# Turning four operands of a chunked recurrence by transpositions where identity products stood

## What is computed

```python
def step(S, inp):
    r_t, w_t, k_t, v_t, a_t, b_t = inp
    sa = jnp.einsum('bhij,bhj->bhi', S, a_t)
    S = S * w_t[:, :, None, :] + sa[..., None] * b_t[:, :, None, :] + v_t[..., None] * k_t[:, :, None, :]
    y = jnp.einsum('bhij,bhj->bhi', S, r_t)
    return S, y
y = _rwkv7_scan(rh, decay, kh, vh, -kk, kk * ah)
```

## Time and profile before

| | us |
|---|---|
| median of three runs | 3031.03 |
| the profiled execution | 3030.16 |
| its span, first to last instruction | 3028.1 |
| PE busy (matmul) | 2707.8 (89%) |
| PE weight loads busy | 2233.2 (74%) |
| DVE / ACT / POOL busy | 1236.1 / 771.9 / 287.3 |
| recurrence, first to last PE instruction | some 265, from 2563 to 2828 |
| TensorE's mean granted clock | 0.944 |

### The profile page before, as it was taken

One profiled execution on the slowest core, in us unless ns is written; L12 is line 12 of the kernel. 1 busy time (PEld: TensorE's weight loads), 2 busy tenths in 40 slices (PEclk: granted clock), 3 DMA queues, 4 the chain that ended last, 5 costly groups with the idle time before them and its releaser, 6 DMA issues. The chain is left out here.

```text
span 3028.1 us, 49010 instructions
## 1 busy us (share of the span) xinstructions
PE 2707.8 (89%) x20661; PEld 2233.2 (74%) x20661; DVE 1236.1 (41%) x2017; ACT 771.9 (25%) x1452; POOL 287.3 (9%) x193
## 2 busy tenths in 40 slices
PE   9799999999987898869999999997998987777766
PEld 8799999999965655758888888875776862676455
DVE  6333333333342567262333333336233334454437
ACT  6221111111151178242111111112211122323221
POOL 1100000000030034020000000005000000222102
PEclk9899999999988999989999999998999996899878
DMA  4211111111036400331111111103202100000032
GB/s 141 77 42 62 43 42 42 42 61 44 22 121 148 166 2 2 114 122 56 42 42 42 62 42 51 54 28 132 71 21 84 49 19 8 4 4 4 4 118 97
DMA packets 59995, 175.92 MB, mean 58 GB/s; under 512 B 10046, under 2 KB 17631, under 8 KB 58672
## 3 DMA queue, kind: packets, MB, share of 16 engines
q1 hardware_dynamic: 59826, 173.47, 17.5%
HBM read 146.50 MB, written 26.36 MB: 57 GB/s over the span
## 5 line engine op out<-in xcount | busy, mean ns | idle before, releaser
L771 PE MATMUL f0gu<-b1XH,f0w0H 128*128 128x346 f32 (+1 forms) x528 | 170.4, 323 | 12.6 <-DVE f0w0L L699 12.6
L773 PE MATMUL f0gu<-b1XH,f0w0L 128*128 128x346 f32 (+1 forms) x528 | 170.6, 323 | 0.0
L725 DVE TENSOR_TENSOR Y<-f0dn,Y 128x512 f32<-128x512 f32 (+1 forms) x180 | 123.9, 689 | 113.7 <-PE f0dn L795 112.7
L772 PE MATMUL f0gu<-b1XL,f0w0H 128*128 128x346 f32 (+1 forms) x528 | 169.9, 322 | 0.0
L773 PE MATMUL f0gu<-b1XH,f0w1L 128*128 128x346 f32 (+1 forms) x528 | 169.7, 321 | 0.0
L771 PE MATMUL f0gu<-b1XH,f0w1H 128*128 128x346 f32 (+1 forms) x528 | 169.3, 321 | 0.0
L714 DVE TENSOR_TENSOR f1hf<-f1sg,f1gu 128x512 f32<-128x512 f32 x44 | 30.2, 687 | 340.4 <-ACT f1sg L667 340.4
L772 PE MATMUL f0gu<-b1XL,f0w1H 128*128 128x346 f32 (+1 forms) x528 | 169.0, 320 | 0.0
L714 DVE TENSOR_TENSOR f0hf<-f0sg,f0gu 128x346 f32<-128x346 f32 (+1 forms) x66 | 34.1, 516 | 329.4 <-ACT f0sg L667 329.4
L771 PE MATMUL f1gu<-b1XH,f1w0H 128*128 128x512 f32 x352 | 139.0, 395 | 12.0 <-DVE f1w0L L699 12.0
L725 DVE TENSOR_TENSOR Y<-f1dn,Y 128x512 f32<-128x512 f32 x160 | 109.2, 690 | 90.6 <-PE f1dn L795 90.6
(11 more groups left out here) (387 smaller groups left out, 6512.2 us busy)
## 6 DMA issues: line engine op xcount, KB each, us to landing
f0raw<-in_w_gate_up SPq DMA_DIRECT2D x44, 512.0 KB, 5.6
f1raw<-in_w_gate_up SPq DMA_DIRECT2D x44, 512.0 KB, 5.2
residual<-Y SPq DMA_DIRECT2D x32, 512.0 KB, 2.8
Y<-in_w_ada SPq DMA_DIRECT2D x8, 1536.0 KB, 6.6
f0rawd<-in_w_down SPq DMA_DIRECT2D x22, 512.0 KB, 3.4
f1rawd<-in_w_down SPq DMA_DIRECT2D x22, 512.0 KB, 3.4
w_in_b_raw<-in_w_in_b SPq DMA_DIRECT2D x17, 512.0 KB, 3.4
w_in_a_raw<-in_w_in SPq DMA_DIRECT2D x12, 512.0 KB, 4.4
```

Source lines behind the costliest of these rows:

```text
L725: dve.tensor_tensor(y, dn[0:r, (par * ND + i) % 4], y, ALU.add).then_inc(s["acc"], 1)
L771: pe.matmul(o, wH[c][:, j, k], xh, start=(k == 0), stop=False)
L772: pe.matmul(o, wH[c][:, j, k], xl, start=False, stop=False)
L773: last = pe.matmul(o, wL[c][:, j, k], xh, start=False, stop=(k == KC - 1))
```

## The change

In `inverse_start` the blocks of chunk 0, whose outputs lie on partitions 0 to 63, become transpositions; those of chunk 1 stay products with the identity. In `turn`, an even head's two chunks become one transposition of a 64x128 block, whose output covers all 128 partitions. An odd head's chunk 1, whose output lies on partitions 0 to 63, becomes a 64x64 transposition; its chunk 0 stays a product. The order within a (pair, operand) is: transposition, transposition, product. Waits and marks stay as they are.

```diff
                         for q in range(2):
                             for e in range(2):
                                 o = H * c
-                                mm = pe.matmul(wk[rows(q), e, o:o + H], XT(t, e, c, q), cst[at(e, q), 1, 0], start=True, stop=True)
+                                if q:
+                                    mm = pe.matmul(wk[rows(q), e, o:o + H], XT(t, e, c, q), cst[at(e, q), 1, 0], start=True, stop=True)
+                                else:
+                                    mm = pe.transpose(wk[rows(q), e, o:o + H], XT(t, e, c, q), cst[at(e, q), 1, 0])
                     pa.mark(mm, "tx")
...
                     for c in range(4):
                         for i, src in enumerate(pair):
-                            for q in range(2):
-                                for e in range(2):
-                                    mm = pe.matmul(wk[at(e, q), e, 4 * H * i + H * c:4 * H * i + H * (c + 1)], src[rows(e), c, chunk(t, q)], b.ident[rows(e), rows(e)], start=True, stop=True)
+                            o = slice(4 * H * i + H * c, 4 * H * i + H * (c + 1))
+                            pe.transpose(wk[:, 0, o], src[rows(0), c, tok(t)], b.ident[rows(0), rows(0)])
+                            pe.transpose(wk[at(1, 1), 1, o], src[rows(1), c, chunk(t, 1)], b.ident[rows(1), rows(1)])
+                            mm = pe.matmul(wk[at(1, 0), 1, o], src[rows(1), c, chunk(t, 0)], b.ident[rows(1), rows(1)], start=True, stop=True)
                     pa.mark(mm, n)
```

## The result

The kernel after takes 3069.02 us (median of 4 runs, 3061.93 to 3078.33), the kernel before 3031.01 (3029.99 to 3035.45). The ratio is 1.0128, with an interval of 1.0112 to 1.0144. It is slower, and the forecast of 3060 us was 9 us short of it. The profiled execution's span is 3068.4 us, 40.3 more than before.

A forecast was written before the change was run, and what follows sets the result against it. PE looked like the bound, stopped mostly by instruction fetch, in blocks of some 253. Seven tiles at +2.8 us (+20) and +9 before the loop made +29, so 3060 us; range 3033 to 3090.

The forecast's parts named there:

- The drain: In turns, each change of array shape costs 0.10 us (0.15 at half clock), making a turn 3.6 us for 0.94.
- Before the loop: For tile 0, at half clock, two turns cost +4 us each and `inverse_start` +1.7, together +9 us.
- The clock: PEclk stays 1.00 in the loop; under 1.00 between 2610 and 2850 would be wrong.
- rival 3: Long turns with a quarter of the array working bring TensorE's clock down: 3073 us, or 3112; chance 0.07.
- its +13 us for the turns' blocks: Half clock only in the two blocks of the turns adds 0.95 us each, over seven tiles: 3073 us.
- The stall as room: Each instruction block's second half leaves 1.3 us of fetch stall, within which longer work costs nothing.
- +2.8 us: Net loss per token tile inside the loop, times seven tiles: +20 us.
- the inverse's 0.7: `inverse_start`'s excess of 1.35 us costs 0.7 us a tile in the loop after the stalls.
- the saving of 2.0: Dropping 144 of 2110 instructions a tile saves 2.0 us per tile, -14 us over seven tiles.
- Rival 1: TensorE overlaps transpositions with products of other shapes, so only the 144 dropped instructions count: 3017 us; chance 0.13.
- Rival 2: Fetch stalls hide the drains, or drains are half as dear, and saved blocks pay: 3025 to 3037 us; chance 0.06.
- The forecast's 0.5 us a tile for such waits: Longer turns swallow 0.5 us a tile of PE's waits on other engines, lowering +3.3 to +2.8 us.

The follow-up runs named there:

- e2_wide_products: Changed kernel's turn order and shapes, but identity products in place of all transpositions, with the old inverse: 3115.48 us, ratio 1.0275 to the kernel before.
- e1_grouped: Changed kernel's turns with all transpositions first, then all products, and the old inverse: 3025.86 us, ratio 0.997 to the kernel before.
- e7_filled: Changed kernel plus three more products in every product phase of a turn, so all four quarters work: 3061.68 us, ratio 1.0095 to the kernel before.
- e11_filled_again: Changed kernel with all four products in each product phase, run again beside the changed kernel on one chip: 3063.34 us, ratio 1.0107 to the kernel before.
- e6_inverse_only: Kernel before with only the inverse's blocks changed, turns left as products: 3029.66 us, ratio 0.9989 to the kernel before.
- e3_all_wide: Turns of transpositions alone from token tile 1 on, odd heads' chunk 0 by a shifted wide one, old inverse: 3018.36 us, ratio 0.9956 to the kernel before.
- e8_wide_both: All-transposition turns plus the changed inverse with its eight transpositions grouped ahead of its eight products: 3018.0 us, ratio 0.9947 to the kernel before.
- e9_double_products: Kernel before with every identity product of the turns issued twice, 256 more instructions a tile: 3053.26 us, ratio 1.0075 to the kernel before.

## Why the prediction came out as it did

- **The drain, right.** 0.10 us for a change of the array's shape came from two kinds of boundary elsewhere in the trace, behind `cum` and in the attention stage. A (pair, operand) was to take 0.45 us and takes 0.45 to 0.46; its phases were 0.19 and 0.26 and are 0.20 and 0.25. A turn was to take 3.6 and takes 3.66. At the half clock 0.75 was forecast, 0.69 measured, 5.6 us a turn for 6.0. `e2_wide_products` shows that the shape is the cause, `e1_grouped` that the order is.
- **Before the loop, right:** +9 forecast, +8.75 measured.
- **The clock, wrong.** The forecast said PEclk 1.00; 0.86 was measured. This is rival 3, to which I gave 0.07, in its mild form: its +13 us for the turns' blocks made 3073, and 3069 was measured. The step that failed is the one that priced a turn at one clock. The rows had the warning in them: full clock with all quarters at work, half clock before the loop with long waits, and a turn of 3.6 us with one quarter at work lies between. I named it and then weighed it as a remote case. It is at least 1.6 us of a tile's loss by one pair of traces and 2.7 by the other, of 5.6 in all. `e7_filled` and `e11_filled_again` show it, as far as a run can that also adds instructions. Rival 3 also says that TensorE stalls a third of the time before; by rows 1 and 2 it is a quarter (52 of 223 us, 6.0 of 22.75).
- **The stall as room, half right.** Per tile, +2.8 us was forecast and +2.9 found with the clock held (`e7_filled`), over six tiles and not seven, and this agreement carries the unknown cost of 192 instructions. If they cost their 2.1 us, the drains and the saved instructions came to under 1 us a tile, and the forecast lay as near to 3069 as it did partly by luck, too much for the drains standing in for the missing clock. No run separates the two. Of the terms in it, the inverse's 0.7 was too large inside the loop (nothing measurable, `e6_inverse_only`), and the saving of 2.0 too, at 144 x 11 ns = 1.6 us.
- **Rival 1, not here:** no change of shape is overlapped. What it would have given, 3017 us, is about what the instructions bring once the alternation is gone: `e3_all_wide` and `e8_wide_both` take 3018, with 160 and 176 instructions fewer a tile for its 144.
- **Rival 2** came true only for the inverse, inside the loop.
- A slip of reading: I gave the recurrence as some 265 us, up to 2828. Its last products end at 2839, so 276. Nothing was computed from it.

The waits of the kernel after, 2605 to 2880, answer rows 5; below them those of `e7_filled`, 2605 to 2865. L2078 and L2080 are the line of `product`, L2074 before.

```profile
PE inv_ps L2092 <- issue: 4.2, 6, 1.1
...
PE inv_ps L2078 <- DVE XX L1941: 2.3, 4, 0.9
```

```profile
PE inv_ps L2080 <- DVE XX L1941: 5.1, 9, 0.9
PE inv_ps L2080 <- issue: 4.6, 6, 1.1
```

"Issue" on one line was 10.4 us, is 4.2 at most in the kernel after and 4.6 at most in `e7_filled`. So longer turns did take the place of fetch stalls, as the forecast had it, and this fits that two turns 2.7 us longer, and an inverse 1.3, cost the tile of `e7_filled` only 2.9 us. The wait for VectorE went from 4.9 to 2.3 in the kernel after, but is 5.1 in `e7_filled`: with the clock held, the drains swallowed none of it. The forecast's 0.5 us a tile for such waits isn't borne out.

## What to carry over

Where small products work in quarters of the array, write instructions of one shape in groups: what counts is how often the shape changes, and a float32 transposition doesn't share the shape of a 64x64 product, even where it is recorded as 64\*64. In this stream a saved instruction was worth some 11 ns, but only where it brought no such changes; regrouped, the same idea made this kernel 0.3 to 0.5% faster where the change as written made it 1.3% slower. And when an edit makes phases like these turns, which are long and leave much of the array idle, price the steps behind them at the half clock too.

## What was not expected of the hardware

- The granted clock falls within a stage in which PE never idles long: 0.86 with the changed turns, 0.82 in `e2_wide_products`, 0.99 with the same transpositions grouped. PE was busy all through these turns (3.66 of 3.66 us), so its busy share doesn't warn of it. What differed before the fall was how much worked between the drains: products in one quarter, against four in `e7_filled`, whose clock stayed at 1.00. No run tells the part of the array from the number of matmuls, which is 32 in a turn of the change and 80 in one of `e7_filled`. In `e2_wide_products` each phase works in half of the array, with 48 matmuls to a turn of 5.06 us, and the clock falls further.
- The second turn of a tile is hit hardest. In the kernel after the clock falls within the first turn in four tiles of seven (their first turns have a mean clock of 0.97, 0.85, 0.86 and 0.82), and the second is then at 0.50 throughout; in the other three it falls only within the second (0.83, 0.93 and 0.96).
- It goes the other way too. Before the loop the kernel before has the half clock, and its turns take 1.99 us for 64 matmuls. In `e9_double_products`, where the first of them is 128 matmuls without a pause, the second is at the full clock, 128 in 2.10 us. In the timeline of PE of `e9_double_products`, the beginning of the first turn and the whole second:

```profile
2575.22 0.71 PE L2060 MATMUL work_ps<-identity,kk 64*64 64x64 f32 x16 [0.71 <-ACT XX L1853]
...
2580.05 2.10 PE L2060 MATMUL work_ps<-identity,PB 64*64 64x64 f32 x128 [1.14 <-ACT tokens_first L1858]
```

- A 64x64 transposition of float32 is recorded as 64\*64 and yet is bordered by drains among 64x64 products (1.82 us for the inverse's 24 matmuls). The recorded shape alone doesn't tell which neighbours can overlap.
- 24 transpositions of 64 columns without a change of shape take 1.16 us, under 0.05 each, faster than the 0.066 to 0.110 that I worked out from rows 8. Here each uses half of the rows of the array, and a transposition of rows 8 all 128 rows or 16.
